# First stage of a two-block transformer kernel: modulation moved from matmuls to vector dot products, and attention heads interleaved with other matmuls

## The reference

```
mod = silu(c) @ w_ada + b_ada            # 1024 -> 6144: shift1, scale1, gate1, shift2, scale2, gate2
h = rms_norm(x, norm1_g) * (1 + scale1) + shift1
c_q, c_kv, k_rope, lru_x, lru_gate, merge_logits = split(h @ w_in)
attn = mla_attention(c_q, c_kv, k_rope, ...)           # 8 heads
rec  = recurrence(conv(lru_x)) * gelu(lru_gate)        # sigmoid gates r and i, decay a = exp(-8 r softplus(-lambda))
g_attn, g_rec = split(sigmoid(merge_logits))
x = x + gate1 * ((g_attn * (attn @ w_o_attn) + g_rec * (rec @ w_o_lru)) @ w_out)
h2 = rms_norm(x, norm2_g) * (1 + scale2) + shift2
x = x + gate2 * peer_ffn(h2)       # 8 heads x 16 of 16384 experts, rows gathered per token
```

## Time and profile before

| what | value |
|---|---|
| median of 3 runs | 1897.32 us (1895.84 to 1901.45) |
| profiled execution, its own time | 1893.44 us |
| its span in the profile | 1891.6 us |
| busy: TensorE matmul | 1563.6 us (83%) |
| busy: VectorE | 785.7 us (42%) |
| busy: ScalarE | 510.1 us (27%) |
| busy: GpSimd | 299.3 us (16%) |
| DMA, mean over the span | 314 GB/s, 594.63 MB |
| mean granted TensorE clock | 0.909 |

### The profile page before, as it was taken

The page is one execution under the profiler, slowest core; times in us unless marked ns, Lnnn a source line. Parts: engine busy times, 40 slices in busy tenths (PEclk is TensorE's granted clock), DMA queues, the critical chain, the costliest instruction groups (busy, mean ns, idle before and its releaser), DMA issues.

```text
span 1891.6 us, 25365 instructions
## 1 busy us (share of the span) xinstructions
PE 1563.6 (83%) x9968; PEld 1224.0 (65%) x9968; DVE 785.7 (42%) x2057; ACT 510.1 (27%) x1284; POOL 299.3 (16%) x260
## 2 busy tenths in 40 slices
PE   3977788977898988989878669989849888888887
PEld 2764566866898887889778636877735445444444
DVE  2173811138677677677675322112161111111112
ACT  2011321023544434444434220021012222222211
POOL 0000000004455444454444100000000000000000
PEclk8988896998899998999999889986969999999999
DMA  9528863329999999999999924331308999999995
GB/s 366 225 98 347 342 247 129 144 82 382 421 420 421 414 420 420 418 418 415 421 419 421 425 120 177 134 134 38 140 1 362 429 429 428 429 428 428 428 429 223
DMA packets 61171, 594.63 MB, mean 314 GB/s; under 512 B 7840, under 2 KB 8096, under 8 KB 8224
## 3 DMA queue, kind: packets, MB, share of 16 engines
q1 hardware_dynamic: 24224, 325.07, 41.8%
q0 software_dynamic: 36864, 268.45, 34.2%
HBM read 592.44 MB, written 1.05 MB: 314 GB/s over the span
## 4 chain that ended last, share of the span: by engine, by line
PE 47%; DMA 33%; DVE 13%; ACT 4%; issue 2%; SPq 1%; POOL 0%; DVEq 0%; ACTq 0%; POOLq 0%
DMA weight_slabs<-in_w_moe 18%; PE bank L554 17%; PE bank L755 12%; DMA gathered_rows<-in_expert_uv,work 9%; PE bank L876 4%; DMA weight_slabs<-in_expert_uv,work 4%; PE bank L783 2%; PE bank L564 2%; DMA weight_slabs<-in_slabs 2%; PE bank L716 2%; DVE gathered_rows L1397 1%; DVE weight_slabs L1495 1%; DVE gathered_rows L1495 1%; PE bank L852 1%; DVE work L1442 1%
## 5 line engine op out<-in xcount | busy, mean ns | idle before, releaser
L755 PE MATMUL bank<-work,weight_slabs 128*128 128x128 f32 x2048 | 278.0, 299 | 82.2 <-ACT work L1083 82.2
L755 PEld LDWEIGHTS bank<-work,weight_slabs 128*128 128x128 f32 x2048 | 270.5, 214 | 93.1 <-ACT work L1083 90.7
L755 PE MATMUL bank<-work,gathered_rows 128*128 128x128 f32 x2048 | 251.3, 279 | 28.6 <-ACT work L1083 28.4
L755 PEld LDWEIGHTS bank<-work,gathered_rows 128*128 128x128 f32 x2048 | 243.1, 194 | 38.7 <-ACT work L1083 36.1
L1146 POOL DMA_INDIRECT gathered_rows<-in_expert_uv,work x128 | 145.6, 1137 | 562.2 <-DVE work L1482 426.6
L554 PE MATMUL bank<-hT,weight_slabs 128*128 128x256 f32 x992 | 219.2, 384 | 4.4 <-ACT hT L943 4.4
L1495 DVE CUSTOM_DVE_ANT_0 gathered_rows<-gathered_rows,work 128x1024 f32<-128x1024 f32 x128 | 156.8, 1227 | 149.9 <-DMA gathered_rows<-in_expert_uv,work 149.9
L554 PEld LDWEIGHTS bank<-hT,weight_slabs 128*128 128x128 f32 x992 | 191.1, 193 | 32.1 <-ACT hT L943 4.6
L1146 POOL DMA_INDIRECT weight_slabs<-in_expert_uv,work x128 | 153.5, 1199 | 199.6 <-PE bank L755 195.3
L876 PE MATMUL bank<-weight_slabs,work 128*32 128x512 f32 x1024 | 131.8, 661 | 61.6 <-DMA weight_slabs<-in_w_moe 60.3
L1495 DVE CUSTOM_DVE_ANT_0 weight_slabs<-weight_slabs,work 128x1024 f32<-128x1024 f32 x128 | 151.3, 1221 | 53.1 <-DMA weight_slabs<-in_expert_uv,work 53.0
(11 more groups left out here) (320 smaller groups left out, 1555.5 us busy)
## 6 DMA issues: line engine op xcount, KB each, us to landing
weight_slabs<-in_w_moe SPq DMA_DIRECT2D x96, 2048.0 KB, 20.6
weight_slabs<-in_slabs SPq DMA_DIRECT2D x55, 2048.0 KB, 11.1
weight_slabs<-in_slabs SPq DMA_DIRECT2D x2, 1024.0 KB, 9.7
gathered_rows<-in_expert_uv,work POOLq DMA_INDIRECT x128, 13.3
weight_slabs<-in_expert_uv,work POOLq DMA_INDIRECT x128, 12.0
weight_slabs<-in_slabs SPq DMA_DIRECT2D x1, 1664.0 KB, 26.7
weight_slabs<-in_slabs SPq DMA_DIRECT2D x1, 1280.0 KB, 11.6
xT<-in_xT SPq DMA_DIRECT2D x1, 1024.0 KB, 5.0
```

The source lines that it names most:

```text
L755: last = nc.tensor.matmul(ps[c // 2][:, (c % 2) * T + t * P:(c % 2) * T + (t + 1) * P], row_at[k][:, D + c * P:D + (c + 1) * P], diag[:, k ...
```

## The change

- **Modulation.** The matmuls, turns and copies of `ada`, `ada_out`, `second_ada` and `ada_columns` go. The slabs of `w_ada` are stored transposed, and `slab_dots` on VectorE takes four 128x1024 dot products per slab against silu(c), broadcast over the partitions (`crow`, which a DMA fills once for each block). The slot is free when the dots are done.
- **Order.** `sscq` moves between lx0 and lx1. lr0 to lr7 come before lg. mg4 to mg7 and yl0 to yl3 move into the attention's loop over heads (`fill`), and with them, on VectorE, one `slab_dots` for each head (ada4 to ada11). bda0 to bda3 are dotted ahead of each `residual`; bda4 to bda11 are loaded among block two's slabs and dotted ahead of its attention. The constants of recurrence and rotation are computed behind `scaled(0)`.
- **Attention.** The weighted values of heads 0 to 3 come at head 4, their turn at head 5; the rest at the end. The q/k norms take one root for both token tiles.
- **Gates.** The input gate and the merge gates are 0.5 (1 + tanh(x/2)), with the 1 added where they are multiplied in; the factors of 0.5 go into the root's scale and into gate1. The reciprocal is of 256 columns, and gates and decays are two loops.
- **Norms.** ScalarE squares x in four parts as `residual` makes them (`x_part`); `sum_squares` and the first matmuls after `modulated` wait chunk by chunk.

```
+    out = wide("ada0", "ada1", "ada2", "ada3") + [("in_small", 8 * (QC + KVC + KRC))] + wide("in_lx0", "in_lx1")
+    out += [("qkv", 2560)] + [("gates", 2048)] + wide("in_lg0", "in_lg1", "in_mg0", "in_mg1")
+    out += wide("in_mg2", "ada4", "ada5", "in_mg3", "ada6", "ada7", "o_lru0", "ada8", "ada9", "o_lru1", "ada10", "ada11")
+    out += wide("o_attn", "w_out0", "w_out1", "bda0", "bda1", "bda2", "bda3", "w_query0") + [("keys", 2048)]
+    out += wide("w_query1", "w_query2", "w_query3")
+    out += wide("in2_0", "in2_1", "in2_2", "in2_3", "in2_4", "in2_5", "bda4", "in2_6", "bda5", "in2_7", "bda6", "bda7", "in2_8",
+                "bda8", "bda9", "in2_9", "bda10", "bda11", "w_pa", "w_pb", "w_o_20", "w_o_21")
...
 # SyncE
+        sp.dma_start(crow[:, :], g["c_row"].partition_broadcast(P)).then_inc(c_in, 16)
         for n, (name, words) in enumerate(SL):
...
+            if slab_before[n] in DOTTED:
+                sp.wait_ge(dots_done, DOTTED.index(slab_before[n]) + 1)
+            if name == "ada1":
+                sp.dma_start(xT[:, :, :], g["xT"]).then_inc(x_in, 16)
...
+            if name == "bda0":
+                sp.wait_ge(dots_done, DOTTED.index("ada11") + 1)
+                sp.dma_start(crow[:, :], g["c_row_2"].partition_broadcast(P)).then_inc(c_in, 16)
...
 # TensorE
+                    if fresh is not None and t == 0:
+                        pe.wait_ge(h_ready, DC * fresh + k + 1)
...
+                if k % 2 == 0:
+                    pe.wait_ge(square_ready, 4 * n + k // 2 + 1)
...
             scores(0)
             for h in range(HEADS):
                 if h + 1 < HEADS:
                     scores(h + 1)
+                if h < HEADS - 1:
+                    fill(h)
+                if h == 4:
+                    weighted(0)
                 b = begin(f"{tag}PT{h}")
...
+                if h == 5:
+                    turn_heads(0)
+            fill(HEADS - 1)
+            weighted(1)
+            turn_heads(1)
...
+        def beside(h):
+            if h < 4:
+                feature_pair(f"mg{4 + h}", slab3(8, 512)(slab(f"in_mg{2 + h // 2}")), T * (h % 2), hT, DC)
+            else:
+                pe.wait_ge(rec_ready, 1)
+                feature_pair(f"yl{h - 4}", slab3(8, 512)(slab(f"o_lru{(h - 4) // 2}")), T * (h % 2), gate, DC)
...
 # VectorE
+        def slab_dots(name):
...
+            dve.wait_ge(silu_ready, 1 + b)
+            dve.wait_ge(slab_loaded[SLOT[n]], slab_value[n])
+            for q in range(4):
+                w = slabs[:, SLOT[n], q * D:(q + 1) * D]
+                ins = V.tensor_tensor_reduce(out=w, in0=w, in1=crow[:, :], scale=1.0, scalar=0.0, op0=ALU.mult, op1=ALU.add,
+                                             accum_out=mod[:, b, at + q:at + q + 1])
+            ins.then_inc(dots_done, 1)
...
+        slab_dots("ada0")
+        dve.wait_ge(consts_in, 32)
+        dve.wait_ge(x_in, 16)
+        stream_norm(0, "ss1", "n1")
+        for i in range(1, 4):
+            slab_dots(f"ada{i}")
+        mod_bias(0, 0)
+        amuls(0, "norm1_g")
+        scaled(0)
...
+        def recurrence_gate(c):
+            dve.wait_ge(emptied["A"], evacs("A", INDEX[f"lr{c}"]))
+            link(V.tensor_scalar(dec[:, c, :], dec[:, c, :], 1.0, None, ALU.add))
+            V.reciprocal(dec[:, c, :], dec[:, c, :]).then_inc(gate_val, 1)
+            V.scalar_tensor_tensor(out=xc[:, c, :], in0=lxm[:, c, :], scalar=1.0, in1=xc[:, c, :], op0=ALU.add, op1=ALU.mult)\
+                .then_inc(input_scale, 1)
...
+            head_in(0)
+            for h in range(HEADS):
+                if h + 1 < HEADS:
+                    head_in(h + 1)
+                fill(h)
+                if h == 4:
+                    heads_out(tag, nth, 0)
             heads_out(tag, nth, 1)
...
+        def beside(h):
+            slab_dots(f"ada{4 + h}")
+            if h in (3, 7):
+                mod_bias(0, 1 + h // 4)
+            if h >= 4:
+                merge_first(f"yl{h - 4}", h - 4, merge[:, 2 * h:2 * h + 2, :])
...
+        for i in range(4):
+            slab_dots(f"bda{i}")
+            residual("xo", 0, i)
```

More of the change, by code:

```diff
@@ L160, in make_plan, with first_fill @@
+    return out
+def first_fill():
+    fill = {h: [(f"mg{4 + h}", "A", [f"in_mg{2 + h // 2}"] if h % 2 else [])] for h in range(4)}
+    for i, h in enumerate((4, 5, 6, 7)):
+        fill[h] = [(f"yl{i}", "D", [f"o_lru{i // 2}"] if i % 2 else [])]
+    return fill
 def make_plan():
[L162 to L164 removed]
@@ L171, in make_plan @@
[L171 to L176 removed]
+    pl += [(f"mg{i}", "A", [f"in_mg{i // 2}"] if i % 2 else []) for i in range(4)]
@@ L943, in modulated, with squares, qk_squares @@
                 A(hT[:, c, :], hT[:, c, :], ACT.Identity, bias=shift[:, c:c + 1]).then_inc(h_ready, 1)
-        def ada_out(name):
-            if name != "ada0":
-                prev = {"ada1": "adaT0", "ada2": "adaT1", "bda0": "adaT2", "bda1": "bdaT0", "bda2": "bdaT1"}[name]
-                act.wait_ge(chunk_ready, INDEX[prev] + 1)
-            freed(A(ada_sb[:, :], take(name)[:, :], ACT.Copy))
-        def second_ada_out(r):
-            ada_out(f"bda{r}")
-            b = take(f"bdaT{r}")
-            freed(A(mod[:, 1, 16 * r:16 * r + 16].rearrange("p (j q) -> p q j", j=4),
-                    b[:, :].rearrange("p (q j x) -> p q j x", q=4, j=4)[:, :, :, 0], ACT.Copy))
-        def attention(tag, hd, nth):
+        def squares(n):
+            for i in range(4):
+                act.wait_ge(x_part, 4 * (n - 1) + i + 1)
+                A(sqx[:, 2 * i:2 * i + 2, :], xT[:, 2 * i:2 * i + 2, :], ACT.Square).then_inc(square_ready, 1)
+        def qk_squares(tag, hd, nth):
             qk = qk1 if hd == HD1 else qk2
@@ L1007, in _ @@
                 freed(A(qk1[:, t, 4 * i:4 * i + 4, :], b[:, 0:384].rearrange("p (h d) -> p h d", h=4), ACT.Copy))
-        attention("a", HD1, 0)
+        act.wait_ge(lru_const, 2)
+        for c in range(DC):
+            act.wait_ge(conv_ready, DC)
+            b = take(f"lr{c}")
+            A(dec[:, c, :], b[:, 0:T], ACT.Exp, bias=small[:, 8, c:c + 1], scale=-1.0)
+            freed(A(lxm[:, c, :], b[:, T:2 * T], ACT.Tanh, bias=small[:, 9, c:c + 1], scale=0.5))
+        qk_squares("a", HD1, 0)
@@ L1009, in _ @@
+        for c in range(DC):
+            act.wait_ge(gate_val, c + 1)
+            act.wait_ge(input_scale, c + 1)
+            A(lxm[:, c, :], dec[:, c, :], ACT.Tanh, scale=small[:, 6, c:c + 1]).then_inc(decay_ready, 1)
+            A(dec[:, c, :], dec[:, c, :], ACT.Exp, scale=small[:, 7, c:c + 1]).then_inc(decay_ready, 1)
         for i in range(4):
             freed(A(gate[:, 2 * i:2 * i + 2, :], take(f"lg{i}")[:, :].rearrange("p (c t) -> p c t", c=2), ACT.Gelu_apprx_tanh))
-        for r in (1, 2):
-            ada_out(f"ada{r}")
@@ new lines, in merge_second, with residual @@
+        def merge_second(name, i, gates):
+            tmp = ytmp[:, i % 2, :].rearrange("p (c t) -> p c t", c=2)
+            freed(name, V.scalar_tensor_tensor(out=tmp, in0=gates, scalar=1.0, in1=pair(take(name)), op0=ALU.add, op1=ALU.mult))
+            link(V.tensor_tensor(yT[i], yT[i], tmp, ALU.add))
+        def residual(name, b, i):
+            bk = take(f"{name}{i}")
+            for q in range(2):
+                c = 2 * i + q
+                ins = V.scalar_tensor_tensor(out=xT[:, c, :], in0=bk[:, q * T:(q + 1) * T], scalar=mod[:, b, 16 + c:17 + c],
+                                             in1=xT[:, c, :], op0=ALU.mult, op1=ALU.add)
+            freed(f"{name}{i}", ins)
+            V.nop().then_inc(x_part, 1)
```

441 lines of the change are left out of this document (193 added, 248 removed).

## The result

| | before | after |
|---|---|---|
| median, runs on the same chip | 1896.58 us (4 runs, 1895.54 to 1901.45) | 1762.74 us (4 runs, 1762.09 to 1763.66) |
| profiled execution, its span | 1893.44, 1891.6 | 1763.66, 1761.8 |
| mean granted TensorE clock | 0.909 | 0.926 |

The ratio is 0.929, with a 95% interval of 0.9273 to 0.9307: faster by 7%. The forecast was 1768, in a range of 1755 to 1802.

The account below looks back on a forecast made before the run. The prediction took TensorE's waits and low clock to bound the first stage, gathers and expert loop being untouched. Nine terms summed to 128.9 us: 1893.44 to 1764.5 profiled, plus 3.9 for a median of 1768, range 1755 to 1802.

Parts of the forecast that it names:

- Start: Block one up to cq, with the first dots on VectorE: cq at 41.6 instead of 44.48, −2.9 us.
- 2 to 5, 7: Waits and modulation work between cq and the attention, −73.8 us, and bda2 behind the attention, −11.0, go.
- step 2: Small norms' sums go ahead of lx1 to lx3: the 14.03 us wait goes, −14.0.
- steps 3, 4, 5 and 7: Modulation leaves TensorE: ada1 and ada2 −30.0 us, bda0 −21.5, bda1 −8.3, bda2 −11.0.
- Attention: First attention with eight mg and yl pairs inside: 79 us instead of 98.5, −19.5 (−9.5 to −21.5).
- The rival of a clock that stays low in pairs between short pieces: Clock stays low in the interleaved attention: +15 to +46 us, total 1783 to 1814; chance 10%.
- Second norm: Between ya and query(0): parts of the square, sum and wait for hT chunks go, −7.2 us (−4 to −8).
- Block two's three terms: Block two's first norm −7.0 us, second norm −5, attention −2.5; together −14.5.
- Margins: Spare time of 4 to 7 us in recurrence, attention's dots, dots ahead of block two's attention, and blocked queue.
- The vector rival: VectorE or slabs late as the margins are overrun: costs 12 to 35 us, total 1780 to 1803; chance 21%.
- Queue: SyncE refills wait for dots, with everything behind them; two loads named have some 7 us to spare.
- The slower rival: In-order refill queue makes each of 20 later modulation slabs cost 9.0 us, 180 in all, total 1948; chance 3%.

Follow-up runs that it names:

- e2: The kernel after with the norms taken whole again (one square of all x, TensorE waiting for all eight chunks of hT): 1791.92 us, ratio 0.9457.
- e1: The kernel before with only the small norms' sums moved between lx0 and lx1: 1879.83 us, ratio 0.9924.
- e3: The kernel after with mg4 to mg7 back ahead of the first attention and yl0 to yl3 behind it: 1784.79 us, ratio 0.9419.
- e10: The kernel of e2 with 7 useless matmuls in the wait ahead of each of the three later sums: 1784.88 us, ratio 0.9402.
- e5: The kernel after with a second reciprocal of 256 columns for each of the recurrence's eight chunks, 14.5 us more on VectorE: 1776.14 us, ratio 0.936.
- e4b: The kernel after with four more 128x1024 passes on VectorE in each head of the first attention: 1790.73 us, ratio 0.9462.

## Why the prediction was right

The sum of the steps gave 1764.5 for the profiled execution, and it took 1763.66. The median was forecast 3.9 above the profiled run, as in the kernel before; here the profiled run lies 0.9 above the median. So most of the 5.3 us between 1768 and 1762.74 is that offset, which belonged to one run and not to the kernel. That the sum came within 0.9 is partly luck: the steps were off by -3.3, -2.2, -0.3, +1.6 and +1.1, the stages taken as unchanged by +2.1, and these errors cancel.

- **Start**, right: cq at 41.33, forecast 41.6, and its 10.06 against 9.96 before. The Trainium skill (TensorE: Matmul & The Clock Gate, "HAM oscillation — how this bites in real kernels") has a group behind a long wait start at the slow clock. The rows agree: cq took 10.06 at a granted clock of 0.70, where a pair at full clock takes 7.07. It did not stay slow for its whole length, and a longer wait cost no more: 20.30 us of idle time cost cq what 4.41 had, and in e2, behind 23.10, it took 8.64.
- **Waits removed (2 to 5, 7)**, right, because nothing else ended later: the window from cq to the attention has no idle time at all, and e1 shows step 2 by itself. For the largest part, the modulation taken off TensorE (steps 3, 4, 5 and 7, 70.8 forecast), no run puts it back; there the rows that are gone and the windows that close behind them are the evidence. The 2.2 beyond the forecast are mostly the up-projection at full clock, which step 2 didn't count: a removed wait also gives back the slow matmuls behind it.
- **Attention**, right in its mechanism, sized 3.3 too small: I took 79 between 77 and 89 as a caution, and it was 75.66. TensorE's own work at full clock was 17.8, estimated 18.9. The rival of a clock that stays low in pairs between short pieces fell: 1.00. The Trainium skill (TensorE: Matmul & The Clock Gate, "A second HAM failure mode: psum-queue depth-cycling") tells of frequent short idles that make the clock fall and rise again. The attentions that stand alone agree as to the fall (0.63 in e3, 0.59 in block two) and not as to the rise. In block two's attention of the kernel after, the clock is 0.94 in the first 8.7 us and then stays at the lower of its two levels, 1.2 GHz of 2.4, to the end:

```profile
1144.00:1176.94 32.94, 27.96 (x102) 20.94 (x101) 9.73 (x28) 10.62 (x36) 0.00 (x0) 0.50 0.32 138
```

  With a pair in each head the same small groups ran at full clock.
- **Second norm**, the one term with a wrong step: I let a quarter of the sum and half of the 3.04 ahead of it stay. The reverse happened. All of the sum stays, 3.62, because TensorE's queue has all 16 of its matmuls behind the last pair; and the whole wait goes, because ScalarE's last quarter is done while the first three are summed. That is 3.04 + 2.70 = 5.7 where the forecast had 7.2. Block two's three terms came to 13.4 for 14.5 by the same step. e2 and e10 add what the trace of before only hinted at, by its sums of 3.72 and 5.28: a wait of 3 us ahead of the sum can cost the clock as well.
- **Margins**, right: the recurrence was forecast about 4 ahead (its own terms, 63 less 58.1, give 4.9) and was 4.9, and e5 found 5.05. VectorE in the attention was forecast at 57 and was 55.60. The vector rival, 21%, didn't come; e4b shows what it would have cost, and that it begins somewhere between 65 and 94 us of VectorE's work.
- **Queue**: from cq to the routing, the gathers aside, TensorE waited for no slab. The slower rival's price of 9 us a slab never arose.

The Trainium skill (Vector Engine (DVE) Microarchitecture Reference, "Points that are easy to get wrong") says that an `S2S2D2_STT` instruction with two sources in SBUF that are not bf16 halves its throughput. No row shows whether the dot product is of that form. It takes 1222 ns for 1024 columns, 1.19 ns a column, and the plain product of 2048 columns at 150.70 took 2.29 us, 1.12 ns a column. A plain product and a `scalar_tensor_tensor` of the same 256 columns, both with two fp32 sources in SBUF and neither with a sum, in the kernel after:

```profile
134.19 0.43 DVE L1444 TENSOR_TENSOR gathered_rows<-work 128x256 f32<-128x256 f32 x1 [0.15 <-DVE gathered_rows L1259]
134.65 0.42 DVE L1445 SCALAR_TENSOR_TENSOR work<-gathered_rows,work 128x256 f32<-128x256 f32 x1
```

No halving against a plain product shows in either.
